# Sample stage: value products with the state rows as moving operand and padded probabilities as stationary one

## The reference, cut to what matters

```python
def _dilated_sample(q, k_all, v_all, n_buf, window, dil, slopes):
    ...
    s = jnp.einsum('bthd,btjhd->bhtj', q, kg).astype(jnp.float32) * A_SCALE + bias[:, None, :]
    s = jnp.where(valid, s, -jnp.inf)
    lse = jax.nn.logsumexp(s, axis=-1)
    p = jnp.exp(s - lse[..., None]).astype(vg.dtype)
    o = jnp.einsum('bhtj,btjhd->bthd', p, vg)      # the value products of this change
    return o, jnp.moveaxis(lse, 1, 2)
```

## Time and profile before

| | us |
|---|---|
| runs | 3661.58, 3672.74, 3659.17 |
| median | 3661.58 |
| profiled execution | 3666.15 |
| its span | 3664.6 |
| PE busy in the span | 3392.5 (93%) |
| DVE, ACT, POOL busy | 1320.5, 1071.3, 665.1 |
| mean granted clock of PE | 0.928 |

### The profile page before, as it was taken

The page is one execution under the profiler, slowest core; times in us unless marked ns, Lnnn a source line. Parts: engine busy times, 40 slices in busy tenths (PEclk is TensorE's granted clock), DMA queues, the critical chain, the costliest instruction groups (busy, mean ns, idle before and its releaser), DMA issues. The chain is left out here.

```text
span 3664.6 us, 48402 instructions
## 1 busy us (share of the span) xinstructions
PE 3392.5 (93%) x18024; PEld 2877.3 (79%) x18024; DVE 1320.5 (36%) x3384; ACT 1071.3 (29%) x2169; POOL 665.1 (18%) x614
## 2 busy tenths in 40 slices
PE   7899999999999999999999489999993999979799
PEld 7777777777778877899999367777772999979787
DVE  5222333222232223123222366666631434533333
ACT  5322222222222222112222245566561111110121
POOL 0000000000000000000000145666573233223200
PEclk9999999999999998999999699999995666779899
DMA  4533123332323331223332200000116676555343
GB/s 137 161 110 123 61 92 116 126 120 64 96 90 111 102 103 45 77 94 123 129 129 91 77 13 19 20 20 20 23 25 206 209 257 229 179 170 205 125 138 118
DMA packets 247520, 398.47 MB, mean 109 GB/s; under 512 B 41160, under 2 KB 200744, under 8 KB 241304
## 3 DMA queue, kind: packets, MB, share of 16 engines
q1 hardware_dynamic: 231448, 234.20, 21.2%
q0 software_dynamic: 15856, 161.36, 12.4%
HBM read 314.78 MB, written 168.80 MB: 132 GB/s over the span
## 5 line engine op out<-in xcount | busy, mean ns | idle before, releaser
L107 PE MATMUL dil_J<-all_xT_hi,dil_w_hi 128*128 128x512 f32 x1152 | 473.2, 411 | 14.7 <-DVE dil_w_lo L712 12.1
L109 PE MATMUL dil_J<-all_xT_hi,dil_w_lo 128*128 128x512 f32 x1152 | 455.2, 395 | 0.0
L108 PE MATMUL dil_J<-all_xT_lo,dil_w_hi 128*128 128x512 f32 x1152 | 454.5, 395 | 0.0
L1313 POOL TENSOR_TENSOR mla_p_lo<-mla_p,mla_p_hi 128x512 fp32r<-128x512 f32 (+1 forms) x320 | 362.4, 1136 | 276.5 <-ACT mla_p_hi L1401 271.6
L107 PE MATMUL gate_ps<-all_xT_hi,gate_w_hi 128*128 128x416 f32 x960 | 339.8, 354 | 9.0 <-DVE gate_w_lo L988 9.0
L108 PE MATMUL gate_ps<-all_xT_lo,gate_w_hi 128*128 128x416 f32 x960 | 337.0, 351 | 0.0
L109 PE MATMUL gate_ps<-all_xT_hi,gate_w_lo 128*128 128x416 f32 x960 | 336.7, 351 | 0.0
L737 DVE CUSTOM_DVE_ANT_0 dil_sm<-dil_S,dil_bias 128x256 f32<-128x256 f32 (+1 forms) x384 | 125.0, 363 | 496.6 <-PE dil_S L829 426.7
L683 ACT ACTIVATE dil_sm<-dil_sm,dil_neg 128x256 f32<-128x256 f32 (+1 forms) x384 | 156.6, 455 | 482.0 <-DVE dil_neg L743 482.0
L107 PEld LDWEIGHTS dil_J<-all_xT_hi,dil_w_hi 128*128 128x128 f32 x1152 | 217.4, 189 | 68.7 <-issue 14.2
L109 PEld LDWEIGHTS dil_J<-all_xT_hi,dil_w_lo 128*128 128x128 f32 x1152 | 216.7, 188 | 50.1
(11 more groups left out here) (284 smaller groups left out, 6526.6 us busy)
## 6 DMA issues: line engine op xcount, KB each, us to landing
out_win_sample<-in_state_win POOLq DMA_DIRECT2D x8, 8128.0 KB, 26.8
smp_kv<-in_state_win SPq DMA_DIRECT2D x72, 512.0 KB
scr_gates<-gate_out POOLq DMA_DIRECT2D x24, 1040.0 KB, 4.7
smp_qb<-scr_hs SPq DMA_DIRECT2D x32, 768.0 KB, 15.7
dil_raw<-in_w_in SPq DMA_DIRECT2D x36, 512.0 KB, 4.0
proj_gm<-scr_gates SPq DMA_DIRECT2D x40, 416.0 KB, 3.3
out_win_sample<-in_state_win POOLq DMA_DIRECT2D x8, 1984.0 KB, 11.4
scr_oa<-dil_rec SPq DMA_DIRECT2D x192, 66.0 KB, 1.6
```

The source lines that it names most:

```text
L107: pe.matmul(out, w[0], x[0], start=first, stop=False)
L108: pe.matmul(out, w[0], x[1], start=False, stop=False)
L109: return pe.matmul(out, w[1], x[0], start=False, stop=last)
L1313: pool.tensor_tensor(pl[b][:, q0:512], p[:, b, q0:512], ph[b][:, q0:512].bitcast(F32), ALU.subtract).then_inc(p_lo, 1)
```

## The change

The roles of the operands are exchanged. The state rows, 128 rows by all 512 channels of a group, are the moving operand; the stationary one is a block of 128x32 of probabilities, in which only the 8 columns of the token at hand are filled and the others are zero. For this, `pT` becomes a buffer of four blocks, set to zero once, into which ACT writes the 8 columns of each token and group. All 12 matmuls of a sequence accumulate in one PSUM tile of 32 rows (token and head) by 512 channels (8 heads of 64). Of these, each row needs only its own head's 64 channels: DVE multiplies the tile by a mask `same` and sums over heads (`totals`), adds the own row, and PE turns the sum in the next sequence at k = 1 (`turn_outputs`), where DVE copies it out (`outputs`).

```diff
--- before.py
+++ after.py
@@ -1701,8 +1701,11 @@
         stat = m.sb("stat", [R, 4])
         own = m.sb("own", [R, 2, HD])
         own3 = m.sb("own3", [R, NG, HD])
-        pT = m.sb("pT", [P, NG, R])
-        ownT = m.sb("ownT", [P, R])
+        STEP = NG * R + H
+        pT = m.sb("pT", [P, DT * STEP])
+        same = m.sb("same", [R, H])
+        diag = m.sb("diag", [R, H, HD])
+        val = m.sb("val", [R, HD])
         oT = m.sb("oT", [P, 4, NS])
         at = m.sb("at", [P, DB], I32)
         atf = m.sb("atf", [P, DB])
@@ -1744,7 +1747,7 @@
         N = m.ps("N", [P, 512])
         OL = m.ps("OL", [P, 512])
         A = m.ps("A", [P, 512])
-        tS, tP, tO, pO = A[:, 0:NG * P], A[:, NG * P:NG * P + NG * R], A[:, NG * P + NG * R:512], A[:, 0:R]
+        tS, tP, pO, tO = A[:, 0:NG * P], A[:, NG * P:NG * P + NG * R], A[0:R, :], A[:, 0:R]
 
         bias_in = m.sem("bias_in")
         row_in, new_in = ([m.sem(f"{n}{f}") for f in range(2)] for n in ("row_in", "new_in"))
...
@@ -1793,7 +1797,7 @@
 
                 for b in range(DB):
                     f = b % 2
-                    waits(sp, own_added, (b - 1) * 3)
+                    waits(sp, own_added, (b - 1) * 2)
                     for which in range(3):
                         for g in range(NG):
                             src = t["hs"][b * DT:(b + 1) * DT, which * QKV + g * AW:which * QKV + (g + 1) * AW]
@@ -1835,6 +1839,7 @@
                 pool.memset(sx[:, NPG:NPG + 1, :], NEG).then_inc(s["ones_set"], 1)
                 for f in range(2):
                     pool.memset(qz[f][:, :, :], 0.0).then_inc(s["zeroed"], 1)
+                pool.memset(pT[:, :], 0.0).then_inc(pT_zeroed, 1)
 
                 def gather(b):
 
@@ -1892,8 +1897,11 @@
                     .then_inc(s["placed"], 1)
                 dve.wait_ge(s["placed"], 1)
                 dve.tensor_copy(at[:, :], atf[:, :]).then_inc(s["at_ready"], 1)
+                dve.tensor_reduce(same[:, :], ident[0:R, 0:R].rearrange("p (k h) -> p h k", h=H), AX.X, ALU.add)\
+                    .then_inc(same_set, 1)
                 dve.wait_ge(s["loaded"], 16 * 9)
                 dve.wait_ge(bias_in, 16)
+                dve.wait_ge(same_set, 1)
                 dve.wait_ge(s["ones_set"], 2)
                 dve.wait_ge(s["zeroed"], 2)
                 dve.wait_ge(s["ql_out"], 1)
...
@@ -1950,26 +1958,35 @@
                     dve.wait_ge(inverted, b + 1)
                     dve.tensor_scalar(sr[:, :], sr[:, :], stat[:, 3:4], None, ALU.mult).then_inc(scaled, 1)
                     dve.wait_ge(scaled, b + 1)
-                    waits(dve, own_turned, b)
                     for g in range(NG):
                         dve.tensor_scalar(own3[:, g, :], row[f][:, 2, g, :], sr[:, NG * P + g:NG * P + g + 1], None,
                                           ALU.mult).then_inc(own_mult, 1)
                     dve.wait_ge(own_mult, (b + 1) * 3)
-                    dve.tensor_tensor(own[:, 0, :], own3[:, 0, :], own3[:, 1, :], ALU.add).then_inc(own_added, 1)
-                    dve.wait_ge(own_added, b * 3 + 1)
-                    dve.tensor_tensor(own[:, 1, :], own[:, 0, :], own3[:, 2, :], ALU.add).then_inc(own_added, 1)
-                    dve.wait_ge(own_added, b * 3 + 2)
-                    dve.tensor_copy(own[:, 0, :], own[:, 1, :]).then_inc(own_added, 1)
+                    dve.tensor_tensor(own3[:, 0, :], own3[:, 0, :], own3[:, 1, :], ALU.add).then_inc(own_added, 1)
+                    dve.wait_ge(own_added, b * 2 + 1)
+                    dve.tensor_tensor(own3[:, 0, :], own3[:, 0, :], own3[:, 2, :], ALU.add).then_inc(own_added, 1)
+
+                def totals(b):
+
+                    dve.wait_ge(pv_ready, (b + 1) * DT)
+                    dve.tensor_tensor(diag[:, :, :], pO.rearrange("p (h d) -> p h d", h=H),
+                                      same[:, :].unsqueeze(2).to_broadcast([R, H, HD]), ALU.mult).then_inc(picked, 1)
+                    dve.wait_ge(picked, b + 1)
+                    dve.tensor_reduce(val[:, :], diag[:, :, :].rearrange("p h d -> p d h"), AX.X, ALU.add)\
+                        .then_inc(summed, 1)
+                    dve.wait_ge(summed, b + 1)
+                    waits(dve, own_turned, b)
+                    for half in range(2):
+                        last = dve.tensor_tensor(own[:, half, :], own3[:, 0, :], val[:, :], ALU.add)
+                    last.then_inc(own_free, 1)
 
                 def outputs(b):
-                    dve.wait_ge(ownT_out, b + 1)
-                    dve.wait_ge(pv_ready, (b + 1) * DT)
+                    dve.wait_ge(own_turned, b + 1)
                     for h in range(2):
                         r = slice(h * HD, (h + 1) * HD)
-                        dve.tensor_tensor(oT[r, :, b * DT:(b + 1) * DT],
-                                          pO[r, :].rearrange("p (k c s) -> p c k s", k=DT, c=4)[:, :, :, h],
-                                          ownT[r, :].rearrange("p (k c s) -> p c k s", k=DT, c=4)[:, :, :, h],
-                                          ALU.add).then_inc(o_added, 1)
+                        dve.tensor_copy(oT[r, :, b * DT:(b + 1) * DT],
+                                        tO[r, :].rearrange("p (k c s) -> p c k s", k=DT, c=4)[:, :, :, h])\
+                            .then_inc(o_added, 1)
 
                 lay_queries(0)
                 for b in range(DB):
@@ -1982,6 +1999,8 @@
                             dots(b, k)
                         if k == (0 if b else DT - 1):
                             dots(b, DT - 1)
+                        if k == 1 and b:
+                            outputs(b - 1)
                         if k == (1 if b else DT - 1):
                             own_scores(b)
                         if k == 3:
@@ -2010,7 +2029,7 @@
                         .then_inc(s["centred"], 1)
                     dve.tensor_tensor(sx[0:DT, NPG, :], sx[0:DT, NPG, :], mb[0:DT, :], ALU.subtract)\
                         .then_inc(s["centred"], 1)
-                    outputs(b)
+                    totals(b)
                     dve.wait_ge(s["exped"], b + 1)
                     dve.tensor_reduce(psumx[:, :], pr[:, :, :].rearrange("p g r -> p r g"), AX.X, ALU.add)\
                         .then_inc(s["p_summed"], 1)
@@ -2023,6 +2042,7 @@
                     dve.wait_ge(s["ol_inverted"], b + 1)
                     dve.tensor_scalar(ol[:, :], OL[0:R, 0:KL], rmax[:, 1:2], None, ALU.mult)\
                         .then_inc(s["ol_scaled"], 1)
+                outputs(DB - 1)
                 dve.wait_ge(gz_in, 16)
                 dve.wait_ge(o_added, 2 * DB)
                 dve.tensor_tensor(us[:, 0:4, :], oT[:, :, :], gz[:, 0:4, :], ALU.mult).then_inc(a_gated, 1)
@@ -2060,11 +2080,12 @@
                             act.activation(sr[:, :], sr[:, :], ACT.Exp, bias=stat[:, 1:2], accum_out=stat[:, 2:3])\
                                 .then_inc(a_exped, 1)
                     act.wait_ge(p_turned, b + 1)
-                    act.wait_ge(own_turned, b + 1)
                     waits(act, pv_ready, b * DT)
-                    act.activation(pT[:, :, :], tP.rearrange("p (g r) -> p g r", g=NG), ACT.Copy).then_inc(pT_out, 1)
-                    waits(act, o_added, b * 2)
-                    act.activation(ownT[:, :], tO, ACT.Copy).then_inc(ownT_out, 1)
+                    if b == 0:
+                        act.wait_ge(pT_zeroed, 1)
+                    act.activation(pT[:, :].rearrange("p (k x) -> p k x", k=DT)[:, :, 0:NG * R]
+                                   .rearrange("p k (g r) -> p k g r", g=NG)[:, :, :, 0:H],
+                                   tP.rearrange("p (g k h) -> p k g h", g=NG, k=DT), ACT.Copy).then_inc(pT_out, 1)
                     act.wait_ge(s["top_turned"], b + 1)
                     act.wait_ge(s["mb_turned"], b + 1)
                     waits(act, s["centred"], b * 2)
@@ -2127,8 +2148,9 @@
                     for g in range(NG):
                         last = pe.transpose(tP[:, g * R:(g + 1) * R], sr[:, g * P:(g + 1) * P], ident[0:R, 0:R])
                     last.then_inc(p_turned, 1)
-                    pe.wait_ge(own_added, b * 3 + 3)
-                    waits(pe, ownT_out, b)
+
+                def turn_outputs(b):
+                    pe.wait_ge(own_free, b + 1)
                     pe.transpose(tO, own[:, :, :].rearrange("p a d -> p (a d)"), ident[0:R, 0:R])\
                         .then_inc(own_turned, 1)
 
@@ -2136,13 +2158,11 @@
                     u = b * DT + tk
                     if tk == 0:
                         pe.wait_ge(pT_out, b + 1)
-                        pe.wait_ge(ownT_out, b + 1)
                     pe.wait_ge(kv_in[u % KVB], kv_count(u))
-                    for c in range(4):
-                        to = tk * H + 2 * c
-                        for g in range(NG):
-                            last = pe.matmul(pO[:, to:to + 2], kv[u % KVB][:, g, 1, c * P:(c + 1) * P],
```

(8 more changed lines are left out.)

7 lines of the change are left out of this document (4 added, 3 removed).

## The result

| | before | changed |
|---|---|---|
| median of 6 runs, us | 3656.91 | 3692.22 |
| lowest to highest | 3651.55 to 3672.74 | 3687.68 to 3698.55 |
| profiled execution, its span | 3666.15, 3664.6 | 3698.55, 3697.0 |
| mean granted clock | 0.928 | 0.925 |

The ratio of the changed kernel to the one before is 1.0085, with a 95% interval of 1.0061 to 1.0109: slower by nearly 1%. The forecast was 3672 within 3635 to 3696, and called a change within 0.5% the likeliest. The time lies in the range, but 20 us over the forecast and over the 3680 that it took as the edge of no change: what came had a chance of about a fifth. The change as forecast by its sum was +6.5 us; measured by the medians it is +35.

What follows compares the result with a forecast made beforehand. The sample stage was taken as bound by PE, with latents set by the DVE and POOL chain; seven periods of 12.6 + 12.9 + 25.5 us, less savings at both ends, gave +6.5 on 3666.15: 3672, range 3635 to 3696.

Steps and rivals of the forecast that it cites:

- The mechanism: Sample stage: some 7 us gained per sequence on matmuls is given back by a longer PE stall and the low clock.
- The rival in which the clock falls no oftener: Turn stretches go low no oftener than now: 3609 if two of seven fall, 3635 if four; chance 0.12, now or better.
- none: Case of the clock rival in which no turn stretch falls low: seven periods 268.1 us, time 3584.
- The rival of padded products that don't lift the clock: Value stretches stay at clock 0.50, 21.0 us each, period 59.4: +76.6 us, 3743; chance 0.05.
- Values: PE's value-product stretch per sequence: 10.3 + 1.9 for lifting the clock + 0.4 = 12.6 us, in place of 20.9 or 19.4.
- the rival of cheap records: Value records aren't two full passes: values 4.8 us shorter per sequence, 38 less in all, 3634; chance 0.03.
- Latents: First latents product to the turned latents, set by DVE's chain: 11.16 + 1.7 = 12.9 us, PE idle some 4.7.
- Turns: Turned latents to the next values: all seven at the low clock, 24.9 + 0.6 = 25.5 us.
- The sum: Seven periods of 51.0 us, +17.8; sequence 0 values -8.3; last latents products -3.0; total +6.5 us.
- The base: The time the sum was added to: the profiled execution's own 3666.15 us, 4.6 over the median.
- Frees of the kv buffers, costed at nothing: kv buffers freed earlier; row loads and the next new queued behind, loads taking some 34 us, less than any period: 0.
- The hinge: Clock at PE's idle time before the turned latents: low after 1.50 and 1.42 us, high after five shorter ones.

Runs made afterwards that it cites:

- fill_ns: Changed kernel with five dummy matmuls on PE ahead of the turned latents and the small own_scores scaling folded into the product before it; 3587 us, ratio 0.9786.
- ctl: The kernel before, unchanged, profiled a second time; 3659 us, ratio 1.0017.
- before_dve: The kernel before with four more VectorE operations, results unused, behind outputs(b), ahead of the latents' scaling; 3720 us, ratio 1.0142.
- no_scalar: Changed kernel with only the small own_scores scaling folded into the product before it, no dummy matmuls; 3684 us, ratio 1.0066.
- fill_pe: Changed kernel with five dummy matmuls on PE in its idle time ahead of the turned latents, scaling kept; 3647 us, ratio 0.9950.

## Why the prediction was right and wrong, point by point

**The mechanism was right.** PE's idle time ahead of the turned latents was forecast as 4.7 us and was 4.4; all seven turn stretches low; the gain on the matmuls given back. The rival in which the clock falls no oftener (3584 to 3635) didn't come. What it is worth when both stalls are gone, fill_ns shows: seven periods of 269.3, where 268.1 had been worked out for "none". That the times, 3587 and 3584, lie as close is in part luck, since the one was measured beside a kernel before of 3667 and the other was worked out from the unlucky execution of 3666. The rival of padded products that don't lift the clock was wrong: values take 12.19 to 13.67 us at 0.79 to 0.90.

**Values**: forecast 12.6, measured 12.7 on average over b = 1 to 7. A record at the high clock was forecast at 0.43 from the 128-column rows and took 0.43, which rules out the rival of cheap records (3634) as well. The 216 ns for one 512-column matmul of the Trainium skill ("TensorE: Matmul & The Clock Gate", Back-to-back issue gap) don't hold for plain f32 here: a matmul is two records and takes 0.86 us.

**Latents**: forecast 12.9, measured 12.71. PE was done 8.3 us after the start of the stretch, for a forecast 8.1; the idle time is the difference, 4.4. `totals` was 0.68 + 1.01 + 0.35 against 0.69 + 0.94 + 0.4; GpSimd's third product shifted along as said, and VectorE waited 1.98 us for it, as before (1.97).

**Turns**: forecast 25.5, measured 26.5. This is the term that was mis-sized, by 1.0 us, seven times. The step was "About the first 1.5 us of it still had the high clock; now that mostly has gone during the idle time: +0.6". From the turned latents to the first L2116 of k = 2 it is 3.90 us now (2956.72 to 2960.62) and was 1.83 before (L2095, 2934.59 to 2936.42), with a transpose of 0.25 in it that moved there from k = 7. At half the clock these records take twice as long, so the loss is all that the high clock had saved, some 1.8 us, less a wait of some 0.3 that was there before. The step took a third of it.

**The sum.** Seven periods: 363.4 - 339.2 = +24.3 against +17.8. Of the 6.4 missed, turns are +7.2, values +0.5 and latents -1.3. Values of sequence 0: -7.3 against -8.3. The end: L2206 of sequence 7 -2.8 against -3.0. The sample stage is thus +14.2 against +6.5; what follows it was 2.8 us shorter.

**The base.** The rest of the miss is in what the sum was added to. In the profile after, the sample stage begins 21 us later, with the same code ahead of it; this is GpSimd's first instruction of the stage, in the changed kernel, then the one before:

```profile
L1838 POOL MEMSET smp_ones<- x1: 98/98/98, 2801.2 to 2801.2; 128x1 f32 x1
```

```profile
L1834 POOL MEMSET smp_ones<- x1: 98/98/98, 2780.2 to 2780.2; 128x1 f32 x1
```

Over the profiles of this study it lies at 2780.2 to 2787.0 in the four kernels with the old products (mean 2782.7) and at 2784.0 to 2801.2 in the ten with the new ones (mean 2788.7). In ctl it lies at 2781.1, within the 3 us of 2780 that ctl's expectation had named as the sign that the changed program makes the stages ahead slower; in before_dve, also with the old products, it lies at 2787.0, later than in four kernels with the new ones. So most of the 21 us is the luck of one execution, some 6 may belong to the new programs, and no run shows by what.

And from that instruction to the end of the span it is 884.4 us in the profile read before but 863.6 in ctl, the same kernel; 895.8 in the changed kernel and 897.9 in no_scalar. The forecast knew this luck ("one turn stretch more or less", which the changed kernel no longer has: its runs lie 11 us apart, those of before 21), yet kept the unlucky 3666 as base, and allowed only +-5 for the other stages. Against the mean of both profiles, 874, the changed stage costs some 22 us, not the 11 that the two profiles read before and after differ by. These 22 and the 6 ahead of the stage are 28 of the 35 us between the medians; the rest isn't accounted for. That the forecast lies only 20 us off is partly luck, owed to the unlucky base: its +6.5 on the median of the six runs before, 3657, would be 3663, 29 us off.

**Frees of the kv buffers, costed at nothing.** Right in time for the changed kernel, and yet not nothing: the product that stands behind the gathers of pages now begins 0.5 to 0.7 us after them, right beside `own_scores`, and that is a stall as soon as PE is at the high clock (fill_pe). In the kernel before it began 5.9 to 8.4 us after them. Longer periods alone don't do that: in before_dve they last 58 us, and it is 3.0 to 7.3 us. That it is the earlier frees is argued from the order of the program and not tested by a run.

**The hinge** was put too sharply: "two of two against five of five" at 1.3 us was a small sample. It didn't matter at 4.4 us; it would have at 1 to 2.

## What to carry to other kernels

When a change makes PE faster next to a chain on another engine, PE's new idle time is the old one plus all that PE gains plus all that the chain gains in length (here 1.05 + 1.8 + 1.55 = 4.4 us). An idle time of 2.6 to 4.4 us cost the high clock every time here, and the work behind it took 1.8 times as long. That and the values entered low make 94 us in seven periods, where the added VectorE instructions by themselves were 12. Look first for what can be taken out of the chain or put in the gap, and test with cheap dummy matmuls in it: the first test shows the next stall, so go on until the periods are what the high clock gives. Taken together the two cheap edits of fill_ns turned 0.9% slower into 2.1% faster. Take the base of a sum from more than one execution where stretches flip between two clocks.
